# Two transformer blocks in one kernel: the order of the second output unit's tiles and the first unit's last tile at the ends of the attention stages

## The reference, cut to what matters

```python
mixed = jnp.concatenate([oa.reshape(b, s, DIFF_WIDTH), ob.reshape(b, s, FOX_WIDTH)], axis=-1)
x = x + rms_norm(mixed @ w_out[l], attn_post_g[l])       # first block, twice
...
o = jnp.transpose(o, (0, 2, 1, 3)).reshape(bsz, seq, D_MODEL)
return o @ w_o                                           # stick-breaking
...
o = o * jax.nn.sigmoid(g)
return o @ w_o                                           # HGRN2
```

## Time and profile before

| | us |
|---|---|
| median of 3 runs | 2707.68 |
| lowest and highest | 2707.38 and 2710.1 |
| the profiled execution | 2704.35 |
| its span, first to last instruction | 2702.6 |
| PE matmuls busy in the span | 2606.3 (96%) |
| DVE busy | 1651.4 (61%) |
| ACT busy | 748.6 (28%) |
| POOL busy | 456.5 (17%) |

### The profile page before, as it was taken

The page is one execution under the profiler, slowest core; times in us unless marked ns, Lnnn a source line. Parts: engine busy times, 40 slices in busy tenths (PEclk is TensorE's granted clock), DMA queues, the critical chain, the costliest instruction groups (busy, mean ns, idle before and its releaser), DMA issues.

```text
span 2702.6 us, 38398 instructions
## 1 busy us (share of the span) xinstructions
PE 2606.3 (96%) x12250; PEld 2058.9 (76%) x12250; DVE 1651.4 (61%) x2625; ACT 748.6 (28%) x1391; POOL 456.5 (17%) x454
## 2 busy tenths in 40 slices
PE   8999899999899989999899989999999999999999
PEld 5776688887577668888766658888888887788887
DVE  6754666454775566645567776544458888564452
ACT  3333232120333333212145541100025555210000
POOL 4111111112111111212201101111211111112111
PEclk9999999999899999999989999999999999999999
DMA  3221233333122123333312113333332221233333
GB/s 110 55 63 53 76 90 100 94 97 99 48 62 63 55 70 98 96 94 101 93 40 63 54 32 93 101 94 95 99 94 63 63 62 47 78 94 101 93 101 94
DMA packets 417270, 214.80 MB, mean 79 GB/s; under 512 B 6819, under 2 KB 416014, under 8 KB 417166
## 3 DMA queue, kind: packets, MB, share of 16 engines
q1 hardware_dynamic: 416144, 212.89, 27.3%
q10 hardware_dynamic: 1022, 0.58, 0.1%
HBM read 211.34 MB, written 2.10 MB: 79 GB/s over the span
## 4 chain that ended last, share of the span: by engine, by line
PE 84%; DVE 7%; ACT 4%; issue 3%; POOL 1%; DVEq 0%; ACTq 0%; POOLq 0%
PE acc L633 71%; PE sc L740 2%; PE sc L1051 1%; PE tp L633 1%; PE tp L763 1%; PE po L786 1%; PE po L633 1%; ACT scratch L1916 1%; ACT scratch L1914 1%; DVE scratch L1440 1%; PE aux L646 1%; PE tp L902 1%; DVE xT L1359 1%; DVE w_lo L1170 1%; PE po L773 0%
## 5 line engine op out<-in xcount | busy, mean ns | idle before, releaser
L633 PE MATMUL acc<-h_hi,w_hi 128*128 128x512 f32 x1968 | 811.0, 412 | 31.0 <-DVE h_lo L1148 24.4
L576 POOL TENSOR_SCALAR w_hi<-w_raw 128x1024 fp32r<-128x1024 f32 x390 | 418.7, 1074 | 2200.4 <-PE acc L633 2130.3
L633 PE MATMUL acc<-h_lo,w_hi 128*128 128x512 f32 x1968 | 775.0, 394 | 0.0
L633 PE MATMUL acc<-h_hi,w_lo 128*128 128x512 f32 x1968 | 775.0, 394 | 0.0
L1170 DVE TENSOR_TENSOR w_lo<-w_raw,w_hi 128x1024 fp32r<-128x1024 f32 x390 | 477.6, 1225 | 76.3 <-POOL w_hi L576 76.2
L633 PEld LDWEIGHTS acc<-h_hi,w_hi 128*128 128x128 f32 x1968 | 373.2, 190 | 142.6 <-issue 40.4
L633 PE MATMUL acc<-mid_hi,w_hi 128*128 128x512 f32 x1120 | 440.4, 393 | 7.3 <-DVE mid_lo L1701 3.2
L633 PE MATMUL acc<-mid_lo,w_hi 128*128 128x512 f32 x1120 | 440.0, 393 | 0.0
L633 PE MATMUL acc<-mid_hi,w_lo 128*128 128x512 f32 x1120 | 438.2, 391 | 0.0
L633 PEld LDWEIGHTS acc<-h_lo,w_hi 128*128 128x128 f32 x1968 | 373.8, 190 | 80.5 <-issue 10.6
L633 PEld LDWEIGHTS acc<-h_hi,w_lo 128*128 128x128 f32 x1968 | 372.8, 189 | 81.6 <-issue 1.4
(11 more groups left out here) (316 smaller groups left out, 2665.1 us busy)
## 6 DMA issues: line engine op xcount, KB each, us to landing
w_raw<-in_mlp_w_dram SPq DMA_DIRECT2D x128, 512.0 KB, 4.1
w_raw<-in_w_in_dram SPq DMA_DIRECT2D x48, 512.0 KB, 3.9
w_raw<-in_w_gate_dram SPq DMA_DIRECT2D x44, 512.0 KB, 3.7
w_raw<-in_w_up_dram SPq DMA_DIRECT2D x44, 512.0 KB, 3.7
w_raw<-in_w_down_dram SPq DMA_DIRECT2D x32, 512.0 KB, 4.1
w_raw<-in_hg_w_in_dram SPq DMA_DIRECT2D x32, 512.0 KB, 4.0
w_raw<-in_sb_w_qkv_dram SPq DMA_DIRECT2D x24, 512.0 KB, 3.8
w_raw<-in_w_out_dram SPq DMA_DIRECT2D x16, 512.0 KB, 4.1
```

The lines of the kernel that those rows point to most:

```text
L576: nc.gpsimd.tensor_scalar(to, w_raw[:, slot], 1.0, 1.0, ALU.mult, ALU.mult).then_inc(w_rounded, 1)
L633: mm = pe.matmul(bank[:], w[:, k], r[:, k], start=(k == 0 and i == 0), stop=(k == k_tiles - 1 and i == 2))
```

## The change

One line of `early_output` changes. Its second list began with a's last tile (3 matmuls) and went on with the 15 matmuls that b had left. Now it begins with b's tiles 3 to 6 (12 matmuls), then come a's last tile (3) and b's last tile (3). The first list, the loop after it, the other engines' lists, the loads and all waits stay as they are.

```diff
                 a, b = (unit(half, i, mid_hi[:, 0], mid_lo[:, 0], ready=ready, base=base) for i in range(2))
                 n = 3 * (KD - 1)
-                return a[:n] + b[:EARLY], a[n:] + b[EARLY:]
+                return a[:n] + b[:EARLY], b[EARLY:n] + a[n:] + b[n:]
```

## The result

The changed kernel is slower. The median of its runs is 2725.05 us (2716.46 to 2725.41, 4 runs) beside 2708.36 us for the kernel before (2707.38 to 2710.1, 4 runs); the ratio is 1.0056, with a 95% interval of 1.0041 to 1.0071. Applied to the 2707.68 us that the forecast started from, that is 15.2 us more, 2722.8 us. The forecast was 10.6 us more, 2718.3 us, and a range of 2711.7 to 2724. By the ratio the result lies in the upper part of the range; the median alone lies 1 us above its upper end. The direction, its place and the order of size were right; one term of the sum, the clock, was too small.

What follows compares the result with a forecast made beforehand. PE's matmuls, busy for 96% of the span, were taken to set the pace, so the four stage ends count. 2 x 2.75 + 0.4 + 0 + 0.7 + 4.0 = 10.6 us on 2707.68 gave 2718.3 us, range 2711.7 to 2724.

Steps and rivals of the forecast that it cites:

- the clock: Loops behind the four new PE waits: each place costs 0 to 1.7 us, taken as 1.0, together 4.0 us.
- No wait to fill in the layers: First block, two layers: a's last tile and the chain to the loop come 2.75 us later, lost in each layer.
- The filled wait of HGRN2 is given back: HGRN2: the 3.18 us wait before a's last tile becomes 3.7 us behind b's last; gain nil.
- rival 3: Not slower: filled waits are won, 2.75 us in HGRN2 and 2.18 in stick-breaking; 2702.8 us, chance 0.04.
- Stick-breaking: Stick-breaking: a's last tile and the split chain to the loop come 0.4 us later, 0.4 us lost.
- POOL's second rounding: It overlaps DVE's L1148 in HGRN2 (0.37 us) and L1143 in each layer (0.17 us); together 0.7 us.
- Rival 1: All four places: the order costs as forecast but the clock does not fall; 6.6 us, 2714.3 us, chance 0.16.
- Rival 2: All four places pay the full clock price, 4 x 1.7 us; 13.4 us in all, 2721.1 us, chance 0.13.

Runs made afterwards that it cites:

- the run with a delay and no pause: Kernel before, plus 15 matmuls whose result nobody reads behind the first two output units in both layers; ratio 1.0018, 4.9 us over before.
- the two partial kernels: The new order in the two layers alone, ratio 1.0035 to the kernel before, and in stick-breaking and HGRN2 alone, 1.0022.
- split first with the order of before: Kernel before, with DVE splitting slot 0's weights directly after taking a's bank in the first pass of the four output loops; ratio 0.9992.
- the two runs with one tile ahead: As split first with the order of before, plus b's tile 3 ahead of a's last tile in stick-breaking and HGRN2; 0.9989 and 0.9992 to before.

## Why the prediction was right, and where its sum was short

**No wait to fill in the layers.** Right. a's last tile came 2.84 us later for 2.75 predicted, the loop 2.89 us later for 2.9. That this is carried to the end of the kernel was an argument from one row; the run with a delay and no pause shows it, 4.9 us for 5.5, within its interval.

**The filled wait of HGRN2 is given back.** Right: 0.45 us left in front (under 0.6 predicted), 3.88 us behind (3.6 to 4.1), nothing won. The split first in DVE's list moved the loop by what it took out of the chain, so the releaser was named correctly, and rival 3 falls with it.

**Stick-breaking.** 0.4 us predicted, about 0.46 read from the rows. One reading was a little off: L946 ends at 1616.47 and not at 1616.3, so a's last tile came 0.70 us behind the data and not 0.5.

**POOL's second rounding.** Right in kind. The term was 0.7 us; the trace shows 0.23 us in HGRN2 and 0.05 and 0.07 in the two layers, so about 0.35. I took two thirds of the overlap from one row (of 0.53 us that is 0.35 and not the 0.37 in the sum). The rows after fit another form better: overlap less 0.15 to 0.22 us. L1143 overlapped by 0.20 us and lost 0.05, L1148 by 0.45 and lost 0.23, L1170 (split first) by 0.97 and lost 0.82; the row of before by 0.48 and lost 0.32; in stick-breaking L1148 overlapped by 0.09 and lost nothing. The rule cited from the Trainium skill, SBUF — State Buffer, Who interferes with whom, that the one blocks the other fully, is borne out by these rows but for that remainder.

**The clock.** This is the term that was too small: "between the two I take 1.0 us", 4.0 us in all. In the profiles of the change, of its repetition and of the two partial kernels there are twelve such places; in ten the loop is longer by about 1.6 us, once by 2.8 us (41.87 less 39.08), and in two it isn't. So a place costs about 1.4 us, 5.7 us for the four. I had averaged the price of one fall, behind 2.18 us, with one wait of 3.18 us that brought none, each read from one execution. Four profiles have these two waits (the kernel before, the new order in the layers alone, the delay without a pause, and split first with the order of before): a fall follows the first in three of them and the second in two, so the two rows were single draws. Behind the new waits of 3.3 to 4.0 us it was ten of twelve; behind the shorter ones of the two runs with the change's order and the split first, two of four at 2.69 us and one of four at 1.87. And in nine of the ten the fall lay wholly behind the loop's start, where it costs its full price. Rival 1 (no fall, 2714.3) lies below the interval of the measured ratio, which is 2718.8 to 2726.9 us. Rival 2 (all pay) was nearer, and so was the rule cited from the Trainium skill, TensorE: Matmul & The Clock Gate, Loop structure matters more than you think, that matmuls behind a long wait run at the lower clock: the rows bear it out in ten of the twelve places. By the runs, the pauses cost 7.3 us (whole change less the kernel with PE kept busy), with an uncertainty of some 5 us, since the two ratios have intervals of 0.15 and 0.11% to either side.

**What stays open.** The order is worth 2 x 2.8 us in the layers, 0.46 and 0.23 in the other two, 6.3 us; with the three falls of 1.6 us in its loops that makes 11.1 of the 12.1 us by which the two first profiles differ. With 5.7 us for the clock it is 12.0 us. The timed runs show 15.2, so of the 4.6 us by which the sum was short the traces account for 1.4. A part of the rest can be seen: the profiled execution of the change is the shortest of its runs, and that of the repetition, with the same program, has a span of 2722.3 us. Its last head of HGRN2, a stage that the change doesn't touch, ran at a mean granted clock of 0.60 (30 us from 2290), against 0.94 in the first profile of the change (from 2288) and 0.89 in the kernel before (from 2276):

```profile
2290.00:2320.00 30.00, 27.42 (x107) 23.66 (x108) 15.45 (x40) 12.60 (x26) 0.00 (x0) 0.60 0.06 16
```

That is no mark of the change: in kernels without its new waits the same stage ran at 0.77 (split first with the order of before, 30 us from 2278), 0.72 and 0.66 (the two runs with one tile ahead, from 2278), and 0.72 (the delay without a pause, from 2284). Whether the change makes such falls more frequent, single profiles can't say; the 3 us lie within the intervals.

## What to carry to other kernels

Before filling a wait with work from behind it, look for what releases the next thing after that work: if it is a chain that starts with the instruction that you let wait, the work was its cover, and the wait only moves behind it. Look at each place where the change applies; here two of four had no wait to fill, and there the filler delayed the head of the chain by its whole length. A new pause of PE costs once more where its clock falls behind it, here by about 1.6 us in ten of twelve places. One row with a fall, or one without, says little of how often it comes: look at several executions before putting a part of the price into a sum.

## What the runs showed of the hardware that was not expected

Two roundings on POOL without a gap (2.05 us) lengthened DVE's split from 1.22 to 2.04 us, and the split was short again (1.23 us) when the second rounding waited for it. The loss follows the overlap less 0.15 to 0.22 us in four kinds of DVE operations, all with two inputs in SBUF. Fourteen matmuls whose result nobody reads, put into waits of 3.3 to 4.0 us, kept the granted clock up in all four places of the profiled execution, for no more than the time of the wait: by the ratios they were worth 0.27% of this kernel, with an uncertainty of 0.2%. And a fall of the clock that a later wait covers costs nothing until that wait is removed: with the split first in the order of before, in the profiled execution, the two falls behind the waits for the last data tile took back most of what the shorter chain had won there.
